# A two-layer mLSTM / GLA decoder step: an earlier first projection, lists of places for the norms, and smaller edits in the mixers

## The reference, cut to what matters

```
for i in range(DEPTH):
    h = rms_norm(x, g_pre_mix[i])
    # mixer: proj = h @ w_in; chunked recurrence; y = gate(o) * head_rms_norm(h, g_head)
    mix = mlstm_mixer(h, ...) or gla_mixer(h, ...)          # ends with y @ w_out
    x = x + rms_norm(mix, g_post_mix[i])
    h = rms_norm(x, g_pre_ffn[i])
    x = x + rms_norm(swiglu(h, w_ffn_gate[i], w_ffn_up[i], w_ffn_down[i]), g_post_ffn[i])
# rms_norm(x, g) = x * rsqrt(mean(x * x) + EPS) * g, over the 1024 features of a token
# swiglu(x) = (silu(x @ w_gate) * (x @ w_up)) @ w_down
# the prompt's states start at zero: C0, n0, m0, S0 = 0
```

## Time and profile before

| what | value |
|---|---|
| median of 3 runs (lowest to highest) | 2768.99 us (2760.65 to 2770.28) |
| the profiled execution, its span | 2773.79 us, 2771.7 us |
| PE, DVE, ACT busy | 96%, 54%, 37% |
| mean granted clock of PE | 0.986 of full speed |
| weights' transfer, 512 KB, issue to landing | 3.5 to 4.1 us (P: 3.7) |
| w_hi on ACT, w_lo on DVE | 1052 ns, 1222 ns |
| one rstd of block 0: ACT Ln and Exp, DVE's three | 689 and 632 ns, 693, 692 and 691 ns |

### The profile page before, as it was taken

One profiled execution on the slowest core, in us unless ns is written; L12 is line 12 of the kernel. 1 busy time (PEld: TensorE's weight loads), 2 busy tenths in 40 slices (PEclk: granted clock), 3 DMA queues, 4 the chain that ended last, 5 costly groups with the idle time before them and its releaser, 6 DMA issues.

```text
span 2771.7 us, 38345 instructions
## 1 busy us (share of the span) xinstructions
PE 2652.2 (96%) x16042; PEld 2392.2 (86%) x16042; DVE 1489.8 (54%) x2286; ACT 1020.4 (37%) x1455; POOL 0.2 (0%) x4
## 2 busy tenths in 40 slices
PE   5999999999999999999999999999999989999996
PEld 3889998877987998789999987998886979999996
DVE  4534455555367663356655676326766377444435
ACT  3443344542334332344433343325343243222222
POOL 0000000000000000000000000000000000000000
PEclk9999999999999999999999999999999999999998
DMA  4455445435323332442332333344225433322222
GB/s 159 140 162 156 129 144 157 132 114 173 126 84 127 106 120 100 153 146 74 106 104 69 115 110 121 125 134 139 90 91 182 133 110 126 111 83 85 77 84 84
DMA packets 181728, 331.25 MB, mean 120 GB/s; under 512 B 19477, under 2 KB 98965, under 8 KB 181557
## 3 DMA queue, kind: packets, MB, share of 16 engines
q1 hardware_dynamic: 181556, 328.81, 36.8%
HBM read 272.48 MB, written 56.28 MB: 119 GB/s over the span
## 4 chain that ended last, share of the span: by engine, by line
PE 83%; DVE 9%; ACT 4%; issue 2%; DMA 2%; SPq 0%; ACTq 0%; DVEq 0%
PE ps L813 75%; PE ps L967 2%; ACT w_hi L1079 1%; DMA w_stage<-w_down_in 1%; DVE Y L1439 1%; DVE n_xs L1442 1%; DVE w_lo L1363 1%; DVE evicted L1391 1%; ACT hid_hi L1136 1%; DVE n_normed L1458 1%; PE ps L908 1%; PE ps L901 1%; PE ps L1042 1%; PE ps L902 1%; PE ps L993 0%
## 5 line engine op out<-in xcount | busy, mean ns | idle before, releaser
L813 PE MATMUL ps<-HH,w_lo 128*128 128x288 f32 (+1 forms) x3696 | 1026.0, 332 | 10.1 <-DVE HL L1454 7.4
L813 PE MATMUL ps<-HH,w_hi 128*128 128x288 f32 (+1 forms) x3696 | 1012.1, 328 | 0.0
L813 PE MATMUL ps<-HL,w_hi 128*128 128x288 f32 (+1 forms) x3696 | 1012.1, 328 | 0.0
L813 PEld LDWEIGHTS ps<-HH,w_lo 128*128 128x128 f32 x3696 | 632.3, 189 | 74.3 <-issue 17.9
L1363 DVE TENSOR_TENSOR w_lo<-w_stage,w_hi 128x1024 fp32r<-128x1024 f32 x396 | 483.8, 1222 | 358.4 <-ACT w_hi L1079 357.5
L813 PEld LDWEIGHTS ps<-HL,w_hi 128*128 128x128 f32 x3696 | 631.1, 189 | 49.5
L813 PEld LDWEIGHTS ps<-HH,w_hi 128*128 128x128 f32 x3696 | 631.2, 189 | 47.3
L1079 ACT ACTIVATE w_hi<-w_stage 128x1024 fp32r<-128x1024 f32 x396 | 416.2, 1052 | 474.9 <-PE ps L813 347.4
L813 PE MATMUL ps<-hid_hi,w_lo 128*128 128x288 f32 (+1 forms) x1056 | 300.8, 340 | 37.9 <-DVE Y L1407 18.0
L1407 DVE TENSOR_TENSOR Y<-ps,Y 128x512 f32<-128x512 f32 (+1 forms) x320 | 227.5, 721 | 153.8 <-PE ps L813 153.0
L813 PE MATMUL ps<-hid_lo,w_hi 128*128 128x288 f32 (+1 forms) x1056 | 293.0, 332 | 0.0
(11 more groups left out here) (191 smaller groups left out, 1618.2 us busy)
## 6 DMA issues: line engine op xcount, KB each, us to landing
w_stage<-w_in_in SPq DMA_DIRECT2D x100, 512.0 KB, 3.7
w_stage<-w_gate_in SPq DMA_DIRECT2D x88, 512.0 KB, 3.5
w_stage<-w_up_in SPq DMA_DIRECT2D x88, 512.0 KB, 3.6
w_stage<-w_down_in SPq DMA_DIRECT2D x88, 512.0 KB, 3.6
w_stage<-w_out_in SPq DMA_DIRECT2D x32, 512.0 KB, 4.1
proj_scratch<-evicted SPq DMA_DIRECT2D x48, 288.0 KB, 2.2
proj_scratch<-evicted SPq DMA_DIRECT2D x48, 256.0 KB, 2.1
x_scratch<-n_xs SPq DMA_DIRECT2D x3, 2304.0 KB, 9.3
```

The costliest lines, as they stand in the source:

```text
L813: mm = pe.matmul(ps[:, grp.bank + t, 0:W], wsl(w, k), x[:, k, t * W:(t + 1) * W], start=(q == 0 and m == 0), stop=(q == len(ks) - 1 and m ...
```

## The change

1. **Start.** x of block 0 comes in eight transfers; HH and HL of the first projection are made of x times the gain, without the norm. The squares and sums follow, the mean stands after unit 2 (rstd 0 1 on P unit 2), and the reciprocal root is multiplied in when block 0's projection leaves PSUM, now by DVE (`late`). The output gates' sigmoid is a step of its own in place; units 22 to 24 open theirs at unit 24. The load of x for block 1 is tagged on P unit 1. The constants come later.
2. **Norms in the FFN.** `ffn_norm` takes a list of places, counted from a U unit, and how many tiles each gets; D units may carry some. It replaces `norm` at norms 3 to 8 (norms 7 and 8 have the lists of 6 and, for the post, 4).
3. **Mixer outputs three slots later** (block 1 of layer 0, block 0 of layer 1).
4. **mLSTM.** Turns of V are a tag of their own, in block 1 one unit after the scores; the samples begin a unit later; the sums of the keys move before the last sample and into another bank.
5. **Gate turns.** Products with the unit matrix (and its negative) become transposes; ACT takes the negative in its Exp.
6. **Zero states.** Chunk 0 of mLSTM and of GLA leaves out the product with the zero state; the state is copied and not added, and the two memsets go.
7. **`la2`.** The last level arguments come after k_decayed and q_decayed.

```diff
-        self.puts(A0[:40])
+        self.puts(A0[:43])
...
-        self.puts(B0[22:46])
+        self.puts(B0[22:49])
...
+    def ffn_norm(sub, blk, start, posts, again=None, pres=()):
+        n = plan.norm[sub, blk].n
+        assert units[start].kind == "U"
+        tag(start, "rstd", n, 0)
+        k = 0
+        for u, tiles in posts:
+            tag(start + u, "post", n, k, k + tiles)
+            k += tiles
+        if again:
+            tag(start + again, "rstd", n, 1)
+            k = 0
+        for u, tiles in pres:
+            tag(start + u, "pre", n, k, k + tiles)
+            k += tiles
...
+    tag(at["P", 0, 0, 1, 0], "xload", 1)
+    tag(at["P", 0, 0, 2, 0], "rstd", 0, 1)
...
-    u = norm(0, 1, u + 1, ones, twos)
+    u = ffn_norm(0, 1, u + 1, ((1, 1), (3, 2), (4, 1), (5, 3), (6, 1)), 8, ((9, 1), (11, 1), (12, 1), (13, 2), (15, 3)))
-    u = norm(1, 0, u + 1, twos, twos)
+    u = ffn_norm(1, 0, u + 1, ((1, 2), (2, 1), (5, 2), (6, 3)), 8, ((11, 3), (12, 1), (13, 4)))
-    u = norm(2, 0, u + 1, twos, twos)
+    u = ffn_norm(2, 0, u + 1, ((1, 2), (3, 1), (5, 3), (7, 2)), 8, ((10, 1), (11, 3), (12, 4)))
-    u = norm(1, 1, u + 1, twos, twos)
+    u = ffn_norm(1, 1, u + 1, ((1, 2), (3, 1), (4, 1), (5, 2), (6, 2)), 8, ((9, 1), (10, 1), (11, 2), (12, 4)))
...
+        tag(a + blk, "mv", c)
...
-    at, ends = ((0, 1, 1, 2, 3, 3, 4, 4), (2, 5)) if layer else ((0, 1, 2, 5, 6, 7, 8, 11), (5, 11))
+    at, ends = ((0, 1, 1, 2, 3, 3, 4, 4), (2, 5)) if layer else ((1, 2, 5, 6, 7, 8, 11, 12), (6, 12))
...
+                if n == 1:
+                    sp.wait_ge(s["summed"], SUM(norms[0].sum1, KD))
...
+                for v in u.opens if u.i >= 17 else [u]:
+                    if v.i >= 17:
+                        sp.wait_ge(s["gained"], v.gained)
+                    else:
+                        sp.wait_ge(s["left_dve" if v.late else "left_act"], v.groups[0].ev)
...
-                        mm = pe.matmul(ps[0:n, M0 + 2, (c * 3 + q) * H:(c * 3 + q + 1) * H], Y[0:H, row, t:t + n],
-                                       g.negi[:, :] if row == 4 else g.ident[0:H, 0:H], start=True, stop=True)
+                        pe.transpose(ps[0:n, M0 + 2, (c * 3 + q) * H:(c * 3 + q + 1) * H], Y[0:H, row, t:t + n],
+                                     g.ident[0:H, 0:H])
...
+                    if c:
+                        pe.matmul(ps[:, M0 + h, 0:DV + 1], g.m.QW[:, h, :], g.C[:, h, :], start=True, stop=False)
+                    mm = pe.matmul(ps[:, M0 + h, 0:DV + 1], g.m.A[:, h, :], g.m.V[:, h, :], start=c == 0, stop=True)
...
+            for k in range(KD):
+                act.wait_ge(s["x_landed"][k], 16)
+                act.activation(g.HH[0][:, k, :], g.n.xs[:, k, 0:NT[0]], ACT.Copy,
+                               scale=g.vec[:, norms[0].pre + k:norms[0].pre + k + 1]).then_inc(s["norm_hi"], 1)
...
+                    dve.scalar_tensor_tensor(E, ps[:, grp.bank, :], scale, R0, ALU.mult, ALU.mult
+                                             ).then_inc(s["left_dve"], 1)
...
             def la2(c):
-                if c < NC:
-                    level_args(c, 3, NLV)
...
+                if c < NC:
+                    level_args(c, 3, NLV)
```

More of the change, by code:

```diff
@@ L59, in __init__ @@
         self.tags = []
+        self.late = kind == "P" and layer == 0 and blk == 0
 class Group:
@@ L180, in norm @@
         return u
-    ones = [(k, k + 1) for k in range(KD)]
+    def ffn_norm(sub, blk, start, posts, again=None, pres=()):
[12 more added lines that the diff above has]
+            k += tiles
+        assert k == KD
+        return start + (pres or posts)[-1][0]
     twos = [(k, k + 2) for k in range(0, KD, 2)]
@@ L240, in schedule @@
     tag(u - 1, "xload", 8)
-    norm(3, 0, u + 1, twos)
+    ffn_norm(3, 0, u + 1, ((1, 2), (2, 1), (5, 2), (6, 3)))
     u = at["D", 1, 1, PAIRS - 1, 1]
@@ L309, in take @@
         return count[what] - 1
-    N[0].sum1, N[0].rstd1, N[0].pre0 = take("sum", 0), take("rstd", 0), take("pre", 0)
+    N[0].sum1, N[0].pre0 = take("sum", 0), take("pre", 0)
     for u in plan.units:
@@ L535, in program, with unit @@
         u.stores = list(stores)
+    def unit(kind, layer, blk, i, j=0):
+        return units[plan.at[kind, layer, blk, i, j]]
     gained = 0
@@ L540, in program @@
             u.gained = gained
-    def unit(kind, layer, blk, i, j=0):
-        return units[plan.at[kind, layer, blk, i, j]]
+            u.opens = [unit("P", 0, 0, i) for i in (22, 23, 24)] if u.late and u.i == 24 else [] if u.late and u.i >= 22 else [u]
     rstds_before = {}
-    n = 1
+    n = 0
     for i, u in enumerate(units):
@@ L571, in xload @@
                 b = N.blk
-                if n and norms[n - 1].pre is not None:
+                if n == 1:
+                    sp.wait_ge(s["summed"], SUM(norms[0].sum1, KD))
+                if norms[n - 1].pre is not None:
                     sp.wait_ge(s["norm_lo"], SUM(norms[n - 1].pre0, 8))
@@ L1019, in ss @@
                     pe.wait_ge(s["half_yn"], 2 * layer + 1)
+                if j == NB - 1 and not layer:
+                    for i in range(H):
+                        mm = pe.matmul(ps[:, M0, 288 + i * NB:288 + (i + 1) * NB], x.KW[0:TS, i, :], g.bmr[:, 0:NB],
+                                       start=True, stop=True)
+                    mm.then_inc(s["keys_summed"], 1)
                 if j % 2 == 0:
@@ L1044, in ss @@
                 mm.then_inc(s["b_state"], 1)
[L1046 to L1059 removed]
+            steps = {"rstd": rstd, "mg4": mgates, "ma": ma, "mv": mv, "mb": mb, "md": md, "me": me, "lg": lgate, "la": la,
+                     "l1": l1, "l2": l2, "lb": lb, "le": le, "ss": ss}
             for n, u in enumerate(units):
+                if n == 4:
+                    pe.wait_ge(s["consts"], 16 * CONSTS)
                 dense(n, u)
@@ L1091, in evict @@
                     grp = u.groups[0]
+                    if u.late:
+                        for v in u.opens if u.i >= 17 else ():
+                            E = g.E[:, v.slot, 0:NT[b]]
+                            act.wait_ge(s["left_dve"], v.groups[0].ev)
+                            act.activation(E, E, ACT.Sigmoid).then_inc(s["opened"], 1)
+                            table["now"] = "gate"
+                        return
                     act.wait_ge(s["groups"], grp.n + 1)
@@ L1487, in mgates @@
                 if j == 0:
-                    dve.wait_ge(s["left_act"], unit("P", 0, blk, 0).groups[0].ev)
+                    dve.wait_ge(s["left_act" if blk else "left_dve"], unit("P", 0, blk, 0).groups[0].ev)
                     step(dve.tensor_scalar(I, GP, g.bi[:, 0:1], None, ALU.add))
@@ L1831, in _ @@
                      "l1": l1, "l2": l2, "lb": lb, "le": le, "ss": ss, "sh": sh}
-            dve.wait_ge(s["consts"], 16 * CONSTS)
             lo(0)
-            sumx(0, 0, KD)
+            dve.wait_ge(s["vec_landed"], 16)
+            for k in range(KD):
+                dve.wait_ge(s["x_landed"][k], 16)
+                dve.wait_ge(s["norm_hi"], k + 1)
+                j = norms[0].pre + k
+                dve.scalar_tensor_tensor(g.HL[0][:, k, :], g.n.xs[:, k, 0:NT[0]], g.vec[:, j:j + 1],
+                                         g.HH[0][:, k, :].bitcast(F32), ALU.mult, ALU.subtract).then_inc(s["norm_lo"], 1)
             lo(1)
-            rstd(0, 1)
-            pre(0, 0, KD)
+            for k in range(KD // 2):
+                add_square(norms[0].sum1, k, 0)
             for n, u in enumerate(units):
+                if n == 4:
+                    dve.wait_ge(s["consts"], 16 * CONSTS)
                 if u.kind != "D" and n + 2 < len(units):
                     lo(n + 2)
-                evict(n, u)
+                if n == 0:
+                    for k in range(KD // 2, KD):
+                        add_square(norms[0].sum1, k, 0)
+                if n == 2:
+                    rstd(0, 1)
+                    evict(0, units[0])
+                    evict(1, units[1])
+                if n >= 2:
+                    evict(n, u)
                 for t in u.tags:
-                    if t[0] in steps:
+                    if t[0] in steps and t[:2] != ("rstd", 0):
                         steps[t[0]](*t[1:])
```

162 lines of the change are left out of this document (86 added, 76 removed).

## The result

The changed kernel takes **2727.4 us** (median of 4 runs, 2725.6 to 2728.0) against 2766.0 for the kernel before in the same comparison: ratio 0.9856, 95% interval 0.9835 to 0.9877. The forecast was 2690, with a range of 2668 to 2718. The direction was right, the gain half of what was forecast: 39 us and not 79. The profiled run of the kernel before (2773.8 us) lies 8 us above its median, so between the two traces the difference is larger, 47 us.

The account below looks back on a forecast made before the run. TensorE (PE) was taken as the bound, busy 2652 of 2771.7 us. Terms -16 - 3.4 - 9 - 5 + 1 - 4.5 + 1 - 43 = -79 gave 2694.8, put at 2690 for the median of runs; range 2668 to 2718.

Parts of the forecast that it names:

- What bounds the kernel: Whole kernel: TensorE (PE) bounds it; clean units take 5.44 us (block 0) or 6.40 us (block 1), which no edit changes.
- The start: First projection: PE starts near 8.8 us but idles 6.9 before unit 5; -16 us, between -25 and -8.
- the term of 2: Start, behind the idle before unit 5: the clock falls, taken to cost 2 us.
- Zero states: Chunk 0 of each layer: 16 records that only multiplied zeros go, at 0.21 us each; -3.4 us.
- Gate turns: Gate turns of both blocks: shorter trains as transposes and no clock fall behind them; -9 us, between -9 and -3.
- V turns: mLSTM turns of V: PE's waits for the previous chunk's gating go; -5 us, between -5 and 0.
- Samples and keys: Layer 0: samples wait 2.4 us, not 1.4 (+1); key sums lose their wait and clock fall (-4.5).
- la2: GLA: waits for k_decayed go, block 0 loses 4.5 us, block 1 gains 4; +1 us, between -8 and +12.
- Lists: Stretches with whole norms: most of 46.8 us of stall and low clock goes; -43 us, between -47 and -25.
- The walk: Norm stretches under the new lists: DVE's work followed place by place, finding little lost; 4 us left for losses.
- Rival (e): D units at the norms: stalls are from ACT's eviction of G, not DVE, and most stay; 2735 us, chance 3%.
- (a): Rival on the norm lists: they only move the stalls, -22 in place of -43; 2711 us, chance 15%.

Follow-up runs that it names:

- e7: The changed kernel with the gate turns as products with the unit matrix again, without the sign: 2729.7 us.
- e4: The kernel before with only the lists of places for norms 3 to 8 and the mixer outputs three slots later: 2754.5 us.
- e6: The changed kernel with GLA's last level arguments ahead of the decayed products again in block 0's chunks only: 2720.5 us.
- e1: The changed kernel with SP's store of x after norms 3 to 7 as its own step, three units after the last post tile: 2694.7 us.
- e15: The kernel before with the norm lists, the later mixer outputs and the store of x three units later: 2724.1 us.

## Why the prediction was wrong, step by step

- **What bounds the kernel**: right. The pitch of 5.44 and 6.40 held in every clean unit.
- **The start, -16**: right in size and way. First product at 7.43 us (forecast 8.8), idle of 7.07 before unit 5 (forecast 6.9), ended by w_lo behind the weights behind x. The low clock after it lasted for one unit, 8.09 us for 5.44 (the term of 2 measured 2.7).

```profile
45.70 0.79 PE L837 MATMUL ps<-HH,w_lo 128*128 128x512 f32 x1 [7.07 <-DVE w_lo L1411]
```

- **Zero states, -3.4**: -4.1; unit 23 also lost an idle of 0.8 ahead of the first product.
- **Gate turns, -9**: -10.6 between these two traces, right, but for a reason too firm: the train is shorter for certain (4.3 us in e7), and the falls that went with it are not in every trace with the same products (e4 has none). The Trainium skill (TensorE: Matmul & The Clock Gate, "Part 4: PE-mode transpose") says that a transpose doesn't count as busy for the clock in the same way; the prediction drew from it that the falls would stay. The granted clock is 1.00 behind both trains, in 11 traces; the measurement decides, for trains as short as these (1.2 and 1.3 us over the unit's pitch).
- **V turns, -5**: -6.5. Three chunks gained 1.4 each and the unit ahead of chunk 8's turns 2.4; the clock behind the old wait was not in the sum.
- **Samples and keys, -3.5**: came out as +3.1 (105.8 to 108.9 us for units 84 to 97). The step that failed is "There DVE first evicts U and makes hid_lo": that w_lo comes before both, and that its weights stand on SP behind a wait and four state loads, wasn't considered: 5.84 us of idle, and not 2.4. The key sums themselves behaved as said: no wait is left.
- **la2, +1**: +0.4 with both halves as forecast, +4.6 in block 0 (idles of 2.9 for ACT's eviction of G) and -4.2 in block 1. In block 0 the size was partly luck: 1.3, 1.5 and 1.8 in chunks 1 to 3 and nothing in chunk 0, where the forecast had 1.1 in all four. e6 shows that the order should differ by block.
- **Lists, -43**: -14.1. The step that failed is "D starts at 947.1 and finds DVE free: nothing lost" and the same step for the other norms. The walk followed DVE tile by tile and was right on DVE: no copy of a first D pair is waited for. But it took the weights, and the w_lo, eviction and hid_lo behind them, to be there, and so put SP's store of 2304 KB, which the last tile of *post* releases, at nothing without a reason. The runs showed 32.7 us in its place (e1: 2727.4 to 2694.7), 28 of it the bytes and 4.6 the wait. Rival (e) came nearest in its number (2735) but named ACT's eviction, which is a symptom in norm 4; (a) had 2711 with DVE's margins and ACT's squares, which the runs clear. With the store out of the way the lists' stretches come to 45 us under the kernel before (their units in e1), and e15 is 42 below it: the term was right for a kernel without that second path.
- **The range**: its upper end, 2718, was rival (a) and a fall or two. The case that two paths run beside each other had no price, and so no place in it.

## What to carry to other kernels

Before a stall is booked as a gain, walk the second path to the same instruction too: here last tile, queue wait, store, weights, split, eviction, 15 us that the kernel before shows in its own trace, at three norms hidden behind the very stall that goes. And ask what a moved step's transfers will newly stand ahead of, as at norm 3. A queue that runs ahead and carries both bulk stores and the stream of weights needs each bulk transfer placed by who stands behind it: tag it apart from the work that produces the data, or cut it in pieces. When two fixes are each worth little, try them together before dropping either.
